# Split fp32r scores in the attention of a one-core transformer layer: query norms moved into the exponential, two scalings per head

## The chip, the cores and the metric

The kernel runs on one core of a Trainium2 chip. The metric is the device time of one launch in microseconds (us); the kernel before has a median of 1211.46 us over three runs (1211.04 to 1212.08).

## The reference, cut to what matters

One layer of width 2048 over 256 tokens, in float32: a norm, a sparse attention with 16 query heads in 4 groups that share a key head, an output projection, a feed-forward of 8192 and a gated addition. What the change touches is the attention:

```python
q = rms_norm(q.reshape(bsz, seq, H, dk), q_g)            # H = 16, dk = 128
k_c = rms_norm(compress(kv(k_c), ...), k_g[0])           # 15 compressed keys
sc = einsum(qb, k_c) * scale;  pc = masked_softmax(sc)   # scale = dk ** -0.5
ss = einsum(qb, kg) * scale;   sw = einsum(qb, kwb) * scale
return gb[0] * o_cmp + gb[1] * o_slc + gb[2] * o_win
```

With 256 tokens both the selected and the window branch see all earlier tokens, so each head has three softmaxes: one over 15 compressed keys, and two causal ones over up to 256 keys (`slc` and `win`, the "two branches").

## The kernel before, in words

Every large product is computed in fp32r, a one-pass float32 format, with both operands split into a high and a low part: three products (hi by hi, hi by lo, lo by hi) stand for one exact one. The weights come in **units** of 128 x 1024 numbers, by SyncE's queue into 8 raw buffers. For each unit ScalarE makes the high part (`split_hi`, L585) and VectorE the low part (`split_lo`, L899) in one of 4 split buffers, and TensorE uses it in two **half-units** (`half_unit`) of six products of 512 columns (`tile_product`, L1373). ScalarE may write unit u only when TensorE has used unit u-4, VectorE follows ScalarE, and TensorE waits for VectorE (`lo_done`).

All other work is written by hand between the units. `split_hi` and `split_lo` are generators: the body under `for k in split_hi(...)` runs on its engine *after* unit k is split and *before* unit k+1. Each engine works strictly in its written order, so what waits in the body holds the next split up.

The attention stands in the projections of the query groups (C_Q+1 to C_Q+3) and in the first 16 units of the output projection. `attention_step(g, s)` says what TensorE does ahead of half-unit s (0 to 15) while group g's queries are prepared and group g-1's heads run; n is 4(g-1):

- s=0, 4: `head_scores` of heads n+2, n+3; s=1, 5, 9: `head_transpose` of n+1 to n+3; s=3, 7, 11: `head_output` of n+1 to n+3
- s=6: the eight transposes of group g's queries, after `normed` (VectorE's scaling by the query norm, `staged_scale`); s=7: `cmp_scores(g)`; s=8, 12: `head_scores` of n+4, n+5; s=13: `head_transpose(n+4)`; s=15: `head_output(n+4)`

Queries `q_t` and keys `k_t` are plain float32. A head's scores are one product of 256 and one of 512 columns (L1512, L1513), each recorded as two MATMULs. Then VectorE masks and takes the maxima (`head_max`, L1058, L1062), ScalarE takes four exponentials (`head_exp`, L662), VectorE scales them by gate over sum (`head_scale`, L1075), TensorE transposes them, ScalarE and VectorE copy them out (`head_pt`: L670, L672 on ScalarE, L1108, L1109 on VectorE), TensorE multiplies with the values (`head_output`, L1560 to L1564), and ScalarE and VectorE split the result (`head_o`: L677, L1114). `cmp_scores` gives the compressed scores of a group, and VectorE's `cmp_max` (L1081, L1084, L1085) masks them, takes maxima and subtracts; the counter `cmp_read` at its end releases ScalarE's `cmp_softmax` and TensorE's `head_scores`. `head_transpose(hh)` waits for `s_scaled` (the end of `head_scale(hh)`) and for `o_done` (the end of `head_o(hh-1)` on VectorE). POOL raises mean squares to the power -1/2 (`power`).

The order on the two engines in the second half of a group's eight units:

```python
# ScalarE, L782-L794                 # VectorE, L1240-L1262
k == 4: head_pt(n+2); head_exp(n+3)  k == 4: head_max(n+3); head_pt(n+2); queries_out(g)
k == 5: head_o(n+2); cmp_softmax(g)  k == 5: head_scale(n+3); head_o(n+2); cmp_max(g)
k == 6: head_pt(n+3); head_exp(n+4)  k == 6: head_max(n+4); head_pt(n+3); cmp_scale(g)
k == 7: head_o(n+3)                  k == 7: head_scale(n+4); head_o(n+3)
```

Later, results are turned by a round trip through DRAM into four buffers (`turned`: the memory of q_t, v_slc, v_win and p_t).

## Time and profile before

| | |
|---|---|
| median of three runs | 1211.46 us (1211.04 to 1212.08) |
| profiled execution, its own time | 1213.45 us |
| its span, first to last instruction | 1211.7 us |
| TensorE (PE) busy | 1203.0 us, 99% |
| VectorE (DVE) busy | 736.6 us, 61% |
| ScalarE (ACT) busy | 573.5 us, 47% |
| granted TensorE clock over the span | 1.00 of full speed |

The attention spans about 184 to 364 us. Times in the trace count from the first instruction. A MATMUL's own duration is longer than what it adds to a row of them, because they are pipelined; what one costs is read from the starts of the instructions around it.

### The profile page before, as it was taken

What the parts mean: (1) busy time and instruction counts of PE and PEld (TensorE: products, weight loads), DVE (VectorE), ACT (ScalarE), POOL (GpSimd) and SP (SyncE); (2) the same over time, 40 slices, a digit from 0 to 9 for tenths busy, and PEclk for the clock granted to TensorE, in tenths of its full rate; (3) what the DMA queues carried; (4) which work ended last, traced back from release to release, by engine and by line L of the source; (5) the groups of instructions that cost most, each with busy time, mean ns of one, the idle gap of its engine ahead of it and who ended that gap; (6) DMA issues with size and microseconds to landing.
All of it is one profiled execution on the core that took longest, in us unless ns stands there. A gap on an engine that the chain in (4) does not pass through costs nothing.

```text
span 1211.7 us, 15271 instructions
## 1 busy us (share of the span) xinstructions
PE 1203.0 (99%) x5499; PEld 992.8 (82%) x5499; DVE 736.6 (61%) x1002; ACT 573.5 (47%) x785; POOL 75.0 (6%) x62
## 2 busy tenths in 40 slices
PE   8999999999999999999999999999999999999998
PEld 7888888888888888888888888888888888888886
DVE  5677646887767646654456564555655457576554
ACT  6554443555455545443344443444433445455442
POOL 1000000000000002100011100011100012000000
PEclk9999999999999999999999999999999999999999
DMA  9677665333338776776667766677666776786661
GB/s 328 199 217 220 179 192 152 112 114 104 105 122 273 216 231 200 242 244 192 192 207 241 247 218 194 179 245 246 222 205 195 206 244 210 250 264 204 210 203 57
DMA packets 159645, 244.85 MB, mean 202 GB/s; under 512 B 11124, under 2 KB 54504, under 8 KB 159592
## 3 DMA queue, kind: packets, MB, share of 16 engines
q1 hardware_dynamic: 159048, 243.63, 64.2%
q8 instruction: 32, 0.52, 0.2%
q10 hardware_dynamic: 544, 0.52, 0.2%
q14 instruction: 21, 0.17, 0.0%
HBM read 230.48 MB, written 13.63 MB: 201 GB/s over the span
## 4 chain that ended last, share of the span: by engine, by line
PE 92%; DVE 4%; DMA 2%; issue 1%; ACT 1%; SPq 0%; ACTq 0%; DVEq 0%
PE acc L1373 84%; DVE w_split L899 1%; PE tr L1429 1%; PE sc L1513 1%; PE sc L1477 1%; PE sc L1526 1%; PE sc L1512 0%; PE sc L1418 0%; PE tr L1418 0%; DMA v_slc<-turn_dram 0%; DMA h<-in_x_dram 0%; DMA q_t<-turn_dram 0%; DMA turn_dram<-junk 0%; DMA turn_dram<-s 0%; PE tr L1561 0%
## 5 line engine op out<-in xcount | busy, mean ns | idle before, releaser
L899 DVE TENSOR_TENSOR w_split<-w_raw,w_split 128x1024 fp32r<-128x1024 f32 x411 | 510.1, 1250 | 396.7 <-ACT w_split L585 396.1
L585 ACT ACTIVATE w_split<-w_raw 128x1024 fp32r<-128x1024 f32 x411 | 431.5, 1058 | 417.8 <-PE acc L1373 413.5
L1373 PE MATMUL acc<-w_split,a_hi 128*128 128x512 f32 x1916 | 598.8, 394 | 0.0
L1373 PE MATMUL acc<-w_split,b_split 128*128 128x512 f32 x1920 | 443.3, 391 | 0.2 <-DVE w_split L899 0.2
L1373 PEld LDWEIGHTS acc<-w_split,b_split 128*128 128x128 f32 x1920 | 359.3, 188 | 77.2 <-issue 2.9
L1373 PEld LDWEIGHTS acc<-w_split,a_hi 128*128 128x128 f32 x1916 | 357.0, 188 | 77.7 <-issue 4.9
L1373 PE MATMUL acc<-w_split,a_lo 128*128 128x512 f32 x958 | 373.5, 390 | 0.0
L1373 PEld LDWEIGHTS acc<-w_split,a_lo 128*128 128x128 f32 x958 | 180.1, 188 | 38.0
L547 POOL TENSOR_TENSOR stage<-stage 128x512 f32<-128x512 f32 x32 | 50.4, 1595 | 559.2 <-ACT stage L593 559.2
L593 ACT ACTIVATE stage<-acc,rstd 128x512 f32<-128x512 f32 x48 | 30.2, 680 | 11.9 <-PE acc L1373 10.2
L533 POOL TENSOR_TENSOR rs<-ms,minus_half 128x8 f32<-128x8 f32 (+1 forms) x7 | 17.4, 2493 | 252.6 <-DVE ms L962 252.6
L662 ACT ACTIVATE s<-s,nmx 128x128 f32<-128x128 f32 (+1 forms) x64 | 28.3, 445 | 5.9 <-DVE nmx L1062 5.9
L1121 DVE TENSOR_TENSOR h<-acc,h 128x512 f32<-128x512 f32 x40 | 25.8, 686 | 7.1 <-PE acc L1373 7.1
L670 ACT ACTIVATE p_t<-tr 128x512 f32<-128x512 f32 x16 | 9.6, 599 | 42.6 <-PE tr L1541 42.6
L1058 DVE CUSTOM_DVE_ANT_0 s<-sc,causal 128x128 f32<-128x128 f32 (+1 forms) x64 | 19.0, 353 | 0.0
L533 POOL TENSOR_TENSOR rstd<-ms,minus_half 128x2 f32<-128x2 f32 x3 | 3.0, 997 | 226.6 <-DVE ms L954 226.6
L1075 DVE TENSOR_SCALAR s<-s,cf 128x128 f32<-128x128 f32 (+1 forms) x64 | 16.1, 317 | 0.6
L1513 PE MATMUL sc<-k_t,q_t 128*128 128x512 f32 x32 | 16.3, 592 | 0.0
L628 ACT ACTIVATE junk_act<-h 128x512 f32<-128x512 f32 x24 | 15.1, 629 | 1.4 <-DVE h L1121 1.0
L913 DVE SCALAR_TENSOR_TENSOR a_lo<-tr,const_t,a_hi 128x256 fp32r<-128x256 f32 x24 | 10.1, 478 | 8.5 <-ACT a_hi L606 8.5
L606 ACT ACTIVATE a_hi<-tr,const_t 128x256 fp32r<-128x256 f32 x24 | 9.5, 474 | 11.1 <-PE tr L1429 11.1
L622 ACT ACTIVATE b_split<-v_win 128x1024 fp32r<-128x1024 f32 x4 | 4.2, 1060 | 18.9 <-DMA v_win<-turn_dram 18.9
(189 smaller groups left out, 504.8 us busy)
## 6 DMA issues: line engine op xcount, KB each, us to landing
w_raw<-in_mlp_w_dram SPq DMA_DIRECT2D x256, 512.0 KB, 4.4
w_raw<-in_nsa_w_in_dram SPq DMA_DIRECT2D x79, 512.0 KB, 4.4
w_raw<-in_nsa_w_out_dram SPq DMA_DIRECT2D x32, 512.0 KB, 3.8
w_raw<-in_ple_w_gate_dram SPq DMA_DIRECT2D x32, 512.0 KB, 4.3
turn_dram<-junk SPq DMA_DIRECT2D x44, 128.0 KB, 3.8
turn_dram<-s SPq DMA_DIRECT2D x44, 128.0 KB, 3.9
w_raw<-in_nsa_cmp_w_dram SPq DMA_DIRECT2D x8, 512.0 KB, 5.1
q_t<-turn_dram SPq DMA_DIRECT2D x12, 256.0 KB, 4.5
```

What stands on the lines that cost most here:

```text
L533: nc.gpsimd.tensor_tensor(o, ms[0:rows, 0:cols], minus_half[0:rows, 0:cols], ALU.pow).then_inc(rs_ready, 1)
L547: nc.gpsimd.tensor_tensor(stage[:, t], stage[:, t], stage[:, t], ALU.mult)\
L585: nc.scalar.activation(w_hi[:, u % SPLIT], w_raw[:, u % RAW], ACT.Copy).then_inc(hi_done, 1)
L593: nc.scalar.activation(dst(t), acc[c % 2][t][:], func, scale=scale[:, t:t + 1])\
L628: ins = nc.scalar.activation(junk_act[:], h[:, t, n * NW:(n + 1) * NW], ACT.Square, accum_out=ss[:, norm, t, n:n + 1])
L662: last = nc.scalar.activation(s, s, ACT.Exp, bias=nmx[:, par, 2 * t + br:2 * t + br + 1], scale=SCALE, accum_out=sm[:, par, 2 * t + br:2 * ...
L899: nc.vector.tensor_tensor(w_lo[:, u % SPLIT], w_raw[:, u % RAW], f32(w_hi[:, u % SPLIT]), ALU.subtract).then_inc(lo_done, 1)
L1058: ins = nc.vector.tensor_tensor_reduce(out=masked, in0=scores, in1=mask, scale=1.0, scalar=-3e38, op0=ALU.add, op1=ALU.max, accum_out=mx[: ...
L1075: ins = nc.vector.tensor_scalar(s, s, cf[:, par, 2 * t + br:2 * t + br + 1], None, ALU.mult)
L1121: nc.vector.tensor_tensor(cols, acc[c % 2][t][:], cols, ALU.add).then_inc(acc_read[c % 2][t], 1)
L1373: last = nc.tensor.matmul(acc[c % 2][t][:], xs[:, kt, toks], ws[:, u % SPLIT, m * NW:(m + 1) * NW], start=(kt == 0 and n == 0), stop=(kt = ...
L1513: nc.tensor.matmul(sc[1][:], q_t[:, j, P:SEQ], keys, start=True, stop=True).then_inc(s_full, 1)
```

## The change

- **Split scores.** Keys become `k_hi` (ScalarE, `keys_hi`) and `k_low` (VectorE); queries become `q_hi` (ScalarE, `queries_hi`, on ScalarE at k == 4 between `head_pt(n+2)` and `head_exp(n+3)`) and `q_lo` (VectorE, `queries_out`, now after ScalarE). A head's scores are three fp32r products of 256 and three of 512 columns. Compressed keys are split side by side (`kc_split`, 16 columns each part): per token half and head one product of 32 columns and one of 16.
- **Queries unscaled.** `staged_scale` of the queries goes. POOL's `power` writes `q_scale` (the norm and the factor in one), which is the scale operand of the exponentials, a pointer to one number a partition in place of a constant. `cmp_max` has five operations in place of three: one adds the second part of the scores, one multiplies by `q_scale`.
- **Order.** `cmp_scores` moves from s=7 to s=8, `head_scores(n+4)` from s=8 to s=9 (behind `head_transpose(n+3)`).
- **Two scalings.** `head_scale` has one multiplication per token half, with the factors broadcast, in place of one per half and branch.
- **Copies.** The 128x256 copy of `head_pt` moves from VectorE to ScalarE.
- **Output product.** The compressed product (fp32r) comes first in its sum, the float32 ones after it.
- **Memory.** Columns 1024 on of x go to `x_late`, whose place `k_low` and then `h_late` take; they are loaded again (1 MB) for `h_late` in the output projection, after all scores. The turns use two buffers in place of four. Small tiles share memory with others.

```diff
@@ keys and queries, ScalarE @@
+            def keys_hi(r, br):
+                for b in range(2):
+                    act.wait_ge(tr_full[b], r + 1)
+                    nc.scalar.activation(k_hi[:, 2 * b:2 * b + 2, :, br],
+                                         tr[b][:].rearrange("p (g t s) -> p g t s", g=2, t=TT), ACT.Copy,
+                                         scale=const_t[:, GAIN_K + 1 + br:GAIN_K + 2 + br]).then_inc(tr_hi[b], 1)
+            def queries_hi(g):
+                for b in range(2):
+                    act.wait_ge(tr_full[b], q_set(g) + 1)
+                    nc.scalar.activation(q_hi[:, 2 * b:2 * b + 2], tr[b][:].rearrange("p (m s) -> p m s", m=2), ACT.Copy,
+                                         scale=const_t[:, GAIN_Q:GAIN_Q + 1]).then_inc(tr_hi[b], 1)
@@ head_exp @@
-                                                    scale=SCALE, accum_out=sm[:, par, 2 * t + br:2 * t + br + 1])
+                                                    scale=q_scale[:, hh // HPG % 2, t, hh % HPG:hh % HPG + 1],
+                                                    accum_out=sm[:, par, 2 * t + br:2 * t + br + 1])
@@ head_pt, ScalarE @@
+                nc.scalar.activation(p_t[:, hh % 2, NW:NW + SEQ], tr[1][:, 0:SEQ], ACT.Copy)
@@ ScalarE, body of unit k @@
-                    if k == 4 and g:
-                        head_pt(n + 2)
-                        head_exp(n + 3)
+                    if k == 4:
+                        if g:
+                            head_pt(n + 2)
+                        if g < G:
+                            queries_hi(g)
+                        if g:
+                            head_exp(n + 3)
@@ queries_out, VectorE @@
-                    dve.wait_ge(tr_full[b], q_set(g) + 1)
-                    nc.vector.tensor_scalar(q_t[:, 2 * b:2 * b + 2], tr[b][:].rearrange("p (m s) -> p m s", m=2),
-                                            const_t[:, GAIN_Q:GAIN_Q + 1], None, ALU.mult).then_inc(tr_done[b], 1)
+                    dve.wait_ge(tr_hi[b], hi_sets(q_set(g)))
+                    nc.vector.scalar_tensor_tensor(
+                        out=q_lo[:, 2 * b:2 * b + 2], in0=tr[b][:].rearrange("p (m s) -> p m s", m=2),
+                        scalar=const_t[:, GAIN_Q:GAIN_Q + 1], in1=f32(q_hi[:, 2 * b:2 * b + 2]),
+                        op0=ALU.mult, op1=ALU.subtract).then_inc(tr_done[b], 1)
@@ head_scale @@
-                    for br in range(2):
-                        s = (s1 if t else s0)[:, par, br]
-                        ins = nc.vector.tensor_scalar(s, s, cf[:, par, 2 * t + br:2 * t + br + 1], None, ALU.mult)
+                    s = (s1 if t else s0)[:, par]
+                    ins = nc.vector.tensor_tensor(s, s, c4[:, t, :, None].to_broadcast([P, 2, (t + 1) * P]), ALU.mult)
@@ cmp_max @@
+                link(nc.vector.tensor_tensor(cmp_s[:], scores[:, :, :, 1, 0:N_CMP], cmp_s[:], ALU.add))
                 rows = cmp_s[:].rearrange("p t j n -> p (t j) n")
                 link(nc.vector.reduce_max(cmp_m[:], rows, axis=AXX))
-                nc.vector.tensor_tensor(rows, rows, cmp_m[:, :, None].to_broadcast([P, TT * HPG, N_CMP]),
-                                        ALU.subtract).then_inc(cmp_read, 1)
+                link(nc.vector.tensor_tensor(rows, rows, cmp_m[:, :, None].to_broadcast([P, TT * HPG, N_CMP]),
+                                             ALU.subtract))
+                dve.wait_ge(rs_ready, 5 + g)
+                own = q_scale[:, g % 2].rearrange("p t j -> p (t j)")[:, :, None]
+                nc.vector.tensor_tensor(rows, rows, own.to_broadcast([P, TT * HPG, N_CMP]), ALU.mult)\
+                  .then_inc(cmp_read, 1)
@@ head_pt, VectorE @@
-                nc.vector.tensor_copy(p_t[:, hh % 2, NW:NW + SEQ], tr[1][:, 0:SEQ])
@@ VectorE, body of unit k @@
-                        if g < G:
-                            staged_scale(4 + g)
@@ head_scores @@
-                keys = k_t[:, g].rearrange("p t b s -> p (t b s)")
-                nc.tensor.matmul(sc[0][:, 0:SEQ], q_t[:, j, 0:P], keys[:, 0:SEQ], start=True, stop=True)
-                nc.tensor.matmul(sc[1][:], q_t[:, j, P:SEQ], keys, start=True, stop=True).then_inc(s_full, 1)
+                for t, cols in ((0, SEQ), (1, NW)):
+                    for n, (qs, ks) in enumerate(three_terms(q_hi, q_lo, *keys(g))):
+                        last = nc.tensor.matmul(sc[t][:, 0:cols], qs[:, j, t * P:(t + 1) * P], ks[:, 0:cols],
+                                                start=(n == 0), stop=(n == 2))
+                last.then_inc(s_full, 1)
@@ cmp_scores @@
-                        nc.tensor.matmul(sc[1][:, at:at + N_CMP], q_t[:, j, t * P:(t + 1) * P], kc_t[:, g],
+                        nc.tensor.matmul(sc[1][:, at:at + 2 * CSTEP], q_hi[:, j, toks],
+                                         kc_split[:, g].rearrange("p b n -> p (b n)"), start=True, stop=False)
+                        last = nc.tensor.matmul(sc[1][:, at:at + CSTEP], q_lo[:, j, toks], kc_split[:, g, 0],
+                                                start=False, stop=True)
@@ attention_step @@
-                        pe.wait_ge(normed, 3 + g)
+                        staged(C_Q + g)
                         transpose_set(q_set(g), from_stage)
-                    if s == 7:
+                    if s == 8:
                         cmp_scores(g)
-                    if s in (8, 12):
+                    if s in (9, 12):
                         head_scores(n + 4 + (s - 8) // 4)
@@ SyncE, output projection @@
+                    if n == 2 and k == 3:
+                        sp.wait_ge(s_full, H)
+                        sp.dma_start(h_late[:], x_v[:, :, 2 * NW:]).then_inc(x_again, 16)
```

## Rows read from the trace of the kernel before

**Rows 1.** First part of the page: busy us (share) by engine.
```profile
PE 1203.0 (99%) x5499; PEld 992.8 (82%) x5499; DVE 736.6 (61%) x1002; ACT 573.5 (47%) x785; POOL 75.0 (6%) x62
```
**Rows 2.** Waits: who waited for whom, total us, times, longest.
```profile
PEld tr L1429 <- DVE p_cmp L1109: 1.2, 3, 0.4
```
**Rows 3.** Chain in order of time: start, us, what; fp32r products without other work.
```profile
80.43 3.83 PE sc L1477 x32
...
241.57 2.75 PE acc L1373 x12
```
**Rows 4.** Timeline (start, us, engine, what): TensorE around the scores of head 2.
```profile
216.32 0.39 PE L1373 MATMUL acc<-w_split,a_lo 128*128 128x512 f32 x1
...
218.31 0.40 PE L1373 MATMUL acc<-w_split,a_lo 128*128 128x512 f32 x1
```
**Rows 5.** Timeline of group 0, queries to the transposes of head 0.
```profile
195.91 1.40 DVE L995 TENSOR_SCALAR q_t<-tr,const_t 128x512 f32<-128x512 f32 x2
...
197.00 0.40 PE L1373 MATMUL acc<-w_split,a_lo 128*128 128x512 f32 x1
...
199.37 0.28 DVE L1081 TENSOR_TENSOR cmp_s<-sc,cmp_neg 128x120 f32<-128x120 f32 x1 [0.94 <-PE sc L1526]
199.69 0.28 DVE L1084 TENSOR_REDUCE cmp_m<-cmp_s 128x8 f32<-128x120 f32 x1
...
208.78 1.01 DVE L1075 TENSOR_SCALAR s<-s,cf 128x128 f32<-128x128 f32 x4
...
210.11 0.27 PE L1540 MATMUL tr<-ident,s 128*128 128x128 f32 x1
```
**Rows 6.** Timeline of group 1, query transposes to the transposes of head 4.
```profile
230.72 0.40 ACT L662 ACTIVATE s<-s,nmx 128x128 f32<-128x128 f32 x1 [0.86 <-DVE nmx L1062]
...
231.39 0.66 PE L1429 MATMUL tr<-ident,stage 128*128 128x128 f32 x4 [0.16 <-DVE p_cmp L1109]
...
231.81 0.70 PE L1373 MATMUL acc<-w_split,a_hi 128*128 128x512 f32 x2
...
232.49 1.05 ACT L585 ACTIVATE w_split<-w_raw 128x1024 fp32r<-128x1024 f32 x1
...
233.57 1.23 DVE L899 TENSOR_TENSOR w_split<-w_raw,w_split 128x1024 fp32r<-128x1024 f32 x1 [0.73 <-ACT w_split L585]
...
234.70 1.85 PE L1526 MATMUL sc<-kc_t,q_t 128*128 128x15 f32 x16
...
236.59 0.28 DVE L1081 TENSOR_TENSOR cmp_s<-sc,cmp_neg 128x120 f32<-128x120 f32 x1
...
241.19 0.17 DVE L1062 TENSOR_SCALAR nmx<-mx 128x4 f32<-128x4 f32 x1
...
244.77 1.23 DVE L899 TENSOR_TENSOR w_split<-w_raw,w_split 128x1024 fp32r<-128x1024 f32 x1 [0.24 <-ACT w_split L585]
...
247.44 0.42 DVE L1114 TENSOR_TENSOR b_split<-tr,b_split 128x256 fp32r<-128x256 f32 x1
...
249.65 0.27 PE L1540 MATMUL tr<-ident,s 128*128 128x128 f32 x1
```
**Rows 7.** Groups of ScalarE by line and shape: busy us, mean ns | idle before.
```profile
L593 ACT ACTIVATE stage<-acc,rstd 128x512 f32<-128x512 f32 x48 | 30.2, 680 | 11.9 <-PE acc L1373 10.2 <-POOL rstd L533 1.4
...
L606 ACT ACTIVATE a_hi<-tr,const_t 128x256 fp32r<-128x256 f32 x24 | 9.5, 474 | 11.1 <-PE tr L1429 11.1
...
L677 ACT ACTIVATE b_split<-tr 128x256 fp32r<-128x256 f32 x12 | 4.6, 386 | 13.5 <-PE tr L1564 13.5
```
**Rows 8.** Groups of VectorE by line and shape.
```profile
L1351 DVE TENSOR_TENSOR h<-stage,h 128x512 f32<-128x512 f32 x7 | 4.8, 692 | 0.2
...
L1351 DVE TENSOR_TENSOR h<-stage,h 128x256 f32<-128x256 f32 x2 | 0.8, 425 | 0.1
```
**Rows 9.** Timeline at the last head (15).
```profile
353.88 0.42 DVE L1114 TENSOR_TENSOR b_split<-sc,b_split 128x256 fp32r<-128x256 f32 x1
...
354.79 0.27 PE L1540 MATMUL tr<-ident,s 128*128 128x128 f32 x1
```

More of the change, by code:

```diff
@@ L153, in sem @@
             return ctx.enter_context(nc.semaphore(name))
-        h = sb("h", [P, TT, D])
+        h_early = sb("h_early", [P, TT, 2 * NW])
+        with nc.sbuf_tensor("x_late", [P, TT, 2 * NW], F32) as x_late:
+            pass
+        with nc.sbuf_tensor("k_low", [P, G // 2, 2 * NW], F32R) as k_low:
+            pass
+        h_late = sb("h_late", [P, TT, 2 * NW])
         a_hi = sb("a_hi", [P, KT, SEQ], F32R)
@@ L178, in trunk_layer @@
         p_cmp = sb("p_cmp", [P, 2, SEQ], F32R)
+        kc_rows, kc_sq = (p_t[0:N_CMP, b, 0:NW] for b in range(2))
         mx = sb("mx", [P, 2, 4])
@@ L279, in trunk_layer @@
         turn_out = [sem(f"turn_out{b}") for b in range(2)]
-        turn_in = [sem(f"turn_in{b}") for b in range(4)]
+        turn_in = [sem(f"turn_in{b}") for b in range(2)]
         turned_hi = sem("turned_hi")
@@ L284, in trunk_layer @@
         blocks = (junk[:], s1[:].rearrange("p a b s -> p (a b s)"))
-        turned = (q_t[:].rearrange("p j s -> p (j s)"), v_slc[:].rearrange("p t n -> p (t n)"),
-                  v_win[:].rearrange("p t n -> p (t n)"), p_t[:].rearrange("p a n -> p (a n)")[:, 0:2 * NW])
+        turned = [v[:].rearrange("p t n -> p (t n)") for v in (v_slc, v_win)]
         block = ctx.enter_context(nc.Block())
@@ L291, in f32, with columns, keys, three_terms @@
             return ap.bitcast(F32)
+        def columns(late, n, t, at=0, cols=NW):
+            at += n % 2 * NW
+            return (late if n >= 2 else h_early)[:, t, at:at + cols]
+        def keys(g):
+            return (k_hi[:, g].rearrange("p t b s -> p (t b s)"), k_low[:, g // 2, g % 2 * NW:(g % 2 + 1) * NW])
+        def three_terms(x_hi, x_lo, y_hi, y_lo):
+            return (x_hi, y_hi), (x_hi, y_lo), (x_lo, y_hi)
         def out_bank(hh):
@@ L504, in _ @@
             nc.gpsimd.memset(fold[:], 0.0)
+            nc.gpsimd.memset(f32(kc_split[:]), 0.0)
             nc.gpsimd.memset(causal[:], 0.0)
@@ L721, in _ @@
                     hidden(0)
+                if k == 7:
+                    keys_hi(R_KS, 0)
             for k in split_hi(CMP_FIRST[1], CMP_UNITS):
@@ L944, in h_rows @@
             def h_rows(n):
-                return lambda t: h[:, t, n * NW:(n + 1) * NW]
+                return lambda t: columns(h_late, n, t)
             def mean_square(n, norm):
@@ L1194, in _ @@
                     dve.wait_ge(kct_full, 1)
-                    nc.vector.tensor_scalar(kc_t[:].rearrange("p g n -> p (g n)"), sc[1][:, 0:G * N_CMP],
-                                            const_t[:, GAIN_K:GAIN_K + 1], None, ALU.mult).then_inc(kct_ready, 1)
+                    own = sc[1][:, 0:G * N_CMP].rearrange("p (g n) -> p g n", n=N_CMP)
+                    kc_hi, kc_lo = (kc_split[:, :, part, 0:N_CMP] for part in range(2))
+                    link(nc.vector.tensor_scalar(kc_hi, own, const_t[:, GAIN_K:GAIN_K + 1], None, ALU.mult))
+                    nc.vector.scalar_tensor_tensor(out=kc_lo, in0=own, scalar=const_t[:, GAIN_K:GAIN_K + 1],
+                                                   in1=f32(kc_hi), op0=ALU.mult, op1=ALU.subtract)\
+                      .then_inc(kct_ready, 1)
                 if k == 6:
@@ L1449, in h_split_by, with from_h @@
                     split_by(r, k % 2)
-            def from_h(n):
-                return lambda t, b: h[:, t, n * NW + b * P:n * NW + (b + 1) * P]
+            def from_h(n, late=h_late):
+                return lambda t, b: columns(late, n, t, b * P, P)
             def staged(c):
@@ L1524, in cmp_scores @@
                     for j in range(HPG):
-                        at = (t * HPG + j) * N_CMP
-                        last = nc.tensor.matmul(sc[1][:, at:at + N_CMP], q_t[:, j, t * P:(t + 1) * P], kc_t[:, g],
-                                                start=True, stop=True)
+                        at, toks = (t * HPG + j) * 2 * CSTEP, slice(t * P, (t + 1) * P)
+                        nc.tensor.matmul(sc[1][:, at:at + 2 * CSTEP], q_hi[:, j, toks],
+                                         kc_split[:, g].rearrange("p b n -> p (b n)"), start=True, stop=False)
+                        last = nc.tensor.matmul(sc[1][:, at:at + CSTEP], q_lo[:, j, toks], kc_split[:, g, 0],
+                                                start=False, stop=True)
                 last.then_inc(cmp_full, 1)
```

106 lines of the change are left out of this document (58 added, 48 removed).

## The prediction

> **What bounds the kernel now.** First the page: TensorE is busy 99% of the span, VectorE 61%, ScalarE 47% [rows 1], so a microsecond less of products is a microsecond less of time, unless TensorE then waits. Second the waits: in the attention the only wait of TensorE that the list charges to another engine more than once is for VectorE's `p_cmp`, 1.2 us in three places [rows 2]. Third the timelines of one group [rows 5, 6], because a busy share says nothing of order. They show how late VectorE's signals come: head 0's scalings end at 208.78 + 1.01 = 209.79 and TensorE takes them at 210.11, 0.32 us later [rows 5]; head 4's transposes start at 249.65, 1.8 us after what they wait for (247.44 + 0.42) [rows 6]; at the last head 0.49 us are left (354.30 to 354.79) [rows 9]. So TensorE is the bound, but a second bound, the ring ScalarE, VectorE, ScalarE, runs 0.3 to 1.8 us behind it. The change takes work off TensorE and puts work on that ring.
>
> **Prices on TensorE.** Fp32r products of 512 columns follow at 2.75/12 = 0.229 us, those of 256 at 3.83/32 = 0.120 [rows 3]; a half-unit is 6 x 0.229 = 1.375. A head's float32 scores stand between two starts that would be three products apart: 218.31 - 216.32 - 3 x 0.229 = 1.30 us [rows 4]. After: 3 x (0.120 + 0.229) = 1.05. That saves 0.25 a head, 16 x 0.25 = 4.0 us. The compressed scores are 16 records of 15 columns in 1.85 us, 0.11 each [rows 6]; after, they are 16 products of 32 or 16 columns, each again with its own 128 weight columns. I take no change (as nearest row; 0.120 each would add 0.13 us a group). The order of the output product and the head's fp32r part cost the same in either place: 0.
>
> Two small waits shrink. In group 0 TensorE's compressed scores come at 199.37 less 16 records, about 0.2 us later than the product at 197.00 would let them, because VectorE's q_t ends at 197.31 [rows 5]; one half-unit more lies between now, so 0.2 goes. The three waits for `p_cmp` (0.4 each) [rows 2]: the copy ahead of `p_cmp` on VectorE goes, which is some 0.34 earlier (425 ns for such a size [rows 8], less the overlap), while TensorE comes 0.25 earlier. 0.4 - 0.34 + 0.25 leaves 0.3; the `staged_scale` ahead of them goes too, so I take 0.15 left and 0.7 us gained of 1.2. TensorE's gains: 4.0 + 0.7 + 0.2 = 4.9 us.
>
> **Prices on the ring.** `cmp_max` gets two operations; such linked ones start 0.32 us apart [rows 5], so +0.63. The exponentials get a pointer for their scale beside the pointer for their bias. No row has two pointers. A copy of 256 columns takes 474 ns with a pointer and 386 without [rows 7], so one pointer costs 0.088; the second costs 0 (both read at once) to 0.088. I take 0.088, as the first did: 4 x 0.088 = +0.35 a head. The Trainium skill, "ScalarE: Activation LUTs", section "What ACT_TABLE_LOAD costs", says that each pointer operand adds about 93 ns; by it alone the term would be 0.37, and no run so far shows a second pointer. `head_scale`: four multiplications take 1.01 us [rows 5]; two tensor-by-tensor ones of 256 and 512 columns take 0.425 + 0.692 less some 0.09 of overlap [rows 8], 1.03: no gain. The 128x256 copy costs ScalarE 0.386 less the overlap, 0.30. `queries_hi` is two passes of 512 columns at 0.68 [rows 7], ahead of `head_exp(n+3)`. `queries_out` keeps its length.
>
> **Group 0, after.** From the start of `cmp_max` to TensorE's transposes of head 0 TensorE needed 210.11 - 199.37 = 10.74 us [rows 5]. One half-unit (1.38) now lies ahead of `cmp_max`, and two heads' scores are 0.25 shorter: 8.86. The ring needed 209.79 - 199.37 = 10.42: `cmp_max`, compressed exponential, ScalarE's split of unit 6, VectorE's, `head_max`, `head_exp`, both splits of unit 7, `head_scale`. Unit 7 stands in it because each engine splits it after the body of unit 6. After: 10.42 + 0.63 + 0.35 = 11.40, and 0.06 to TensorE. TensorE waits 11.46 - 8.86 = 2.6 us (part of it at head 0's scores, for `cmp_read`, the rest at the transposes).
>
> **Groups 1 to 3, after.** From the end of the query transposes to those of head 4 TensorE takes 249.65 - 231.81 = 17.84; the same steps in another order, less two times 0.25, make 17.34. The ring from the landing of the transposes (231.39 + 0.66 = 232.05) [rows 6]:
> - `queries_hi`, second bank, 0.04 + 0.68 - 0.09 (overlap) = 0.63. Before, `head_exp` ran at 230.72 and waited for no queries.
> - `head_exp`, 232.49 - 230.72 = 1.77, + 0.35 = 2.12; ScalarE's split to VectorE's split, 233.57 - 232.49 = 1.08
> - VectorE's split, `head_scale`, `head_o` to `cmp_max`: 236.59 - 233.57 = 3.02
> - `cmp_max` to the end of the next head's `nmx`, 241.36 - 236.59 = 4.77, + 0.63 = 5.40
> - 0.04 + `head_exp` 2.12 + ScalarE's split 1.08; VectorE's split to the end of `head_o`, 247.86 - 244.77 = 3.09; 0.06 to TensorE
>
> The sum: 0.63 + 2.12 + 1.08 + 3.02 + 5.40 + 2.16 + 1.08 + 3.09 + 0.06 = 18.64. TensorE's clock starts at 231.81, 0.24 before the ring's at 232.05, so it arrives at 17.34 - 0.24 = 17.10. It waits 18.64 - 17.10 = 1.54 us a group, 4.6 us for three. Behind the waiting transposes stand all later products, so the wait is lost time.
>
> **The last head.** 0.49 us were left [rows 9]. The copy (0.30) and the pointer (0.35) make the ring 0.65 longer, which is 0.2 of wait at least. The ring's round for one head also becomes about as long as TensorE's (some 8.85 us each), so lateness carried in from earlier is not made up; I take 0.9, with 0.2 to 1.1 as bounds.
>
> **The sum.** Gains 4.9; waits 2.6 + 4.6 + 0.9 = 8.1; net +3.2 us. Against the profiled execution's own 1213.45 (1.75 beyond its span of 1211.7) this is 1216.6; the median of the runs is 1.99 below that execution, so the forecast is 1211.46 + 3.2 = 1214.7.
>
> **What is costed at nothing, and its cover.** ScalarE's `keys_hi` (two times 1.3 us) runs at k = 7 while TensorE is over two half-units from the next unit; without that cover it would cost up to 1.3 each. The second load of x is twice a unit's load, issued when all scores are made, and VectorE needs it only when the third output chunk ends, some 14 units (38 us) later; SyncE's queue waits for the last scores at the time at which it would wait for a split buffer anyway, and eight raw buffers cover it. Two turn buffers in place of four: VectorE writes the blocks of turn n after it has read turn n-1, so the new owner is never early. The extra clearing of `kc_split` on POOL delays only TensorE's first filler products, which end before the loads of x.
>
> **Rivals.**
> - *The second pointer is free.* Every ring passes one `head_exp` (group 0) or two (groups 1 to 3). Waits: 2.6 - 0.35, 3 x (1.5 - 0.7), 0.5: 5.2. Net +0.3, 1211.8, no difference. For it: no row shows two; against it: the 88 ns of one.
> - *TensorE's saving comes through (the other side).* The ring has cover that my sums do not see: VectorE or ScalarE pick up their splits earlier, and the waits total under 2.5 us, from where on it is faster by over 0.2%. With none, -4.9, 1206.6. For it: TensorE is the bound today with 0.3 to 1.8 us to spare. Against it: group 0's wait alone is 2.6, built of measured stretches.
> - *A transfer or a turn gets in the way.* The reload or the halved turns make one wait of about 3 us more: 1217.7. For it: SyncE's queue is one and in order; against it, the covers above.
>
> **Chances.** My forecast 0.60, the free pointer 0.25, the saving 0.12, the transfer 0.03. About 0.2%, 2.4 us, is what a measurement tells from no change. The forecast's own range is 1213.2 to 1217.2 (last head 0.2 to 1.1, up to 0.3 us a ring for hops that I read 0.1 off); nearly all of it is slower, the free pointer is no difference. So slower 0.60, same 0.28, faster 0.12. The range reaches down past the free pointer: 1210.5 to 1217.5.
>
> **What would show it.** Right: in the list of waits TensorE's transposes of heads 0, 4, 8, 12 wait for VectorE's scaling or `b_split`, head 0's over 1.5 us; the first piece of `head_exp`, 0.40 us now [rows 6], takes 0.49; scores cost 1.05 us between starts; `head_scale` stays at 1.0 us. Wrong if that piece still takes 0.40, or if TensorE's waits in the attention total under 5 us.

## Result, and the profile after

Five runs of the changed kernel have a median of 1216.89 us (1215.83 to 1218.31); the kernel before, over five runs as well, 1212.01 (1211.04 to 1213.16). The ratio is 1.0039, with a 95% interval of 1.0028 to 1.0051: slower by 4.9 us by the medians, 3.4 to 6.2 by the interval. Forecast were 1214.7 us, which is 3.2 more than the 1211.46 of the first three runs of the kernel before, and a range of 1210.5 to 1217.5.

The profiled execution took 1215.83 us, with a span of 1213.7. The busy times of the page answer [rows 1]:

```profile
PE 1199.8 (99%) x5531; PEld 994.5 (82%) x5531; DVE 729.2 (60%) x959; ACT 589.7 (49%) x813; POOL 71.5 (6%) x63
```

TensorE is busy 3.2 us less than before, ScalarE 16 us more, and yet the time grew. The list of waits, TensorE's own lines (who waited for whom, total us, times, longest), answers [rows 2]:

```profile
PE tr L1605 <- DVE b_split L1172: 2.3, 4, 0.6
PE sc L1659 <- POOL ident L537: 2.2, 1, 2.2
PE tr L1605 <- DVE s L1131: 2.0, 1, 2.0
PE sc L1574 <- DVE cmp_s L1146: 1.2, 3, 0.4
PE tr L1490 <- DMA h_early<-in_x_dram: 1.0, 1, 1.0
PE tr L1625 <- DVE p_cmp L1167: 0.3, 2, 0.2
```

Before, one wait of the attention was listed, 1.2 us for `p_cmp` ahead of the query transposes. It is gone. In its place stand four groups: the transposes of heads 0, 4, 8, 12 and 15 wait for the scaling (L1131) or for the low part of the output (L1172, `o_done`), the scores of heads 4, 8 and 12 for the compressed maximum (L1146), and the outputs of heads 3, 7 and 11 for `p_cmp` (L1167; the list has two of these three, the starts show all). These figures are idle time only. A MATMUL's record is longer than the time it adds to a row of them, so what a wait costs is read from the starts, as the timeline of group 1 shows (start, us, engine, line, what, idle before); it answers the second half of [rows 6]:

```profile
240.16 0.28 DVE L1146 TENSOR_TENSOR cmp_s<-cmp_s,q_scale 128x120 f32<-128x120 f32 x1
240.47 0.30 ACT L724 ACTIVATE cmp_s<-cmp_s 128x120 f32<-128x120 f32 x1 [4.36 <-DVE cmp_s L1146]
...
240.59 0.36 PE L1574 MATMUL sc<-k_hi,q_split 128*128 128x256 f32 x1 [0.39 <-DVE cmp_s L1146]
...
240.68 1.04 ACT L612 ACTIVATE w_split<-w_raw 128x1024 fp32r<-128x1024 f32 x1
...
241.76 1.23 DVE L950 TENSOR_TENSOR w_split<-w_raw,w_split 128x1024 fp32r<-128x1024 f32 x1 [1.32 <-ACT w_split L612]
...
242.90 0.28 DVE L1112 CUSTOM_DVE_ANT_0 s<-sc,causal 128x128 f32<-128x128 f32 x1
...
244.13 0.16 DVE L1117 SCALAR_TENSOR_TENSOR nmx<-mx,q_scale 128x4 f32<-128x4 f32 x1
...
244.33 0.49 ACT L703 ACTIVATE s<-s,nmx,q_scale 128x128 f32<-128x128 f32 x1 [1.59 <-DVE nmx L1117]
...
245.88 0.59 ACT L703 ACTIVATE s<-s,nmx,q_scale 128x256 f32<-128x256 f32 x1
...
246.46 1.04 ACT L612 ACTIVATE w_split<-w_raw 128x1024 fp32r<-128x1024 f32 x1
...
247.54 1.23 DVE L950 TENSOR_TENSOR w_split<-w_raw,w_split 128x1024 fp32r<-128x1024 f32 x1 [1.21 <-ACT w_split L612]
...
249.29 1.02 DVE L1131 TENSOR_TENSOR s<-s,cf 128x256 f32<-128x256 f32 x2
...
249.85 0.39 PE L1434 MATMUL acc<-w_split,a_lo 128*128 128x512 f32 x1
250.23 0.42 DVE L1172 TENSOR_TENSOR b_split<-tr,b_split 128x256 fp32r<-128x256 f32 x1
...
250.79 0.30 PE L1605 MATMUL tr<-ident,s 128*128 128x128 f32 x1 [0.56 <-DVE b_split L1172]
```

The last product before head 4's transposes starts at 249.85, so they could start at 250.08; they start at 250.79, 0.71 later, and read against the same transposes without a wait, which add 0.88 us to the row of products, the place costs 0.75. Read so, each of the three full groups loses 0.65 (scores), 0.40 (output) and 0.75 (transposes), 1.8 us; group 0 loses 0.42 at head 0's scores and 2.26 at its transposes (from 208.38, the start of the last product, to 210.81, theirs); the last head 0.83: 8.9 us in all. Read the same way, the kernel before loses 1.6 us: 1.17 in the three waits for `p_cmp` and 0.4 in group 0.

The rows also show how the ring is built. ScalarE stands 4.36 us at the compressed exponential (L724), with the split of unit 6 behind it. VectorE stands 1.32 us for that split, with the maximum of head 4 (L1112) behind it. Then ScalarE takes the exponential and only after it splits unit 7 (246.46), VectorE waits 1.21 us for that, with the scaling (L1131) behind it, and TensorE waits for the scaling.

### The profile page after: what moved, and what is told of

Its sections match the earlier page's. It is cut to its first block, busy times and chain, and to the rows that moved or that the text cites. A ratio compares the mean times of both kernels' runs of the same rounds, so it can differ in the third digit from the quotient of the medians.

```text
span 1213.7 us, 15318 instructions
## 1 busy us (share of the span) xinstructions
PE 1199.8 (99%) x5531; PEld 994.5 (82%) x5531; DVE 729.2 (60%) x959; ACT 589.7 (49%) x813; POOL 71.5 (6%) x63
## 4 chain that ended last, share of the span: by engine, by line
PE 91%; DVE 5%; ACT 3%; issue 1%; DMA 0%; ACTq 0%
PE acc L1434 86%; DVE w_split L950 2%; ACT s L703 2%; ACT w_split L612 1%; PE tr L1490 1%; DVE s L1131 1%; PE sc L1538 1%; DVE s L1112 1%; PE sc L1574 1%; PE sc L1479 0%; PE tr L1479 0%; DMA h_early<-in_x_dram 0%; PE acc L1464 0%; ACT q_split L688 0%; DVE b_split L1172 0%
## 5 line engine op out<-in xcount | busy, mean ns | idle before, releaser
L703 ACT ACTIVATE s<-s,nmx,q_scale 128x128 f32<-128x128 f32 (+1 forms) x64 | 34.2, 537 | 11.9 <-DVE nmx L1117 11.9
L649 ACT ACTIVATE b_split<-v_slc 128x1024 fp32r<-128x1024 f32 x8 | 8.5, 1061 | 31.0 <-DMA v_slc<-turn_dram 31.0
L649 ACT ACTIVATE b_split<-v_win 128x1024 fp32r<-128x1024 f32 x8 | 8.5, 1060 | 26.9 <-DMA v_win<-turn_dram 26.9
L1574 PE MATMUL sc<-k_hi,q_split 128*128 128x256 f32 (+1 forms) x64 | 18.6, 343 | 1.3 <-DVE cmp_s L1146 1.2
L1112 DVE CUSTOM_DVE_ANT_0 s<-sc,causal 128x128 f32<-128x128 f32 (+1 forms) x64 | 18.9, 350 | 0.0
L560 POOL TENSOR_TENSOR q_scale<-ms,minus_half 128x8 f32<-128x8 f32 x4 | 7.5, 1862 | 175.1 <-DVE ms L1013 175.1
L1131 DVE TENSOR_TENSOR s<-s,cf 128x256 f32<-128x256 f32 (+1 forms) x32 | 16.4, 554 | 0.6
L993 DVE TENSOR_TENSOR b_split<-v_win,b_split 128x1024 fp32r<-128x1024 f32 x8 | 16.5, 2063 | 0.0
L1179 DVE TENSOR_TENSOR h_late<-acc,h_late 128x512 f32<-128x512 f32 x20 | 12.9, 686 | 3.9 <-PE acc L1434 3.9
L1179 DVE TENSOR_TENSOR h_early<-acc,h_early 128x512 f32<-128x512 f32 x20 | 12.9, 686 | 3.3 <-PE acc L1434 3.3
```

The costliest lines, as they stand in the source:

```text
L649: nc.scalar.activation(b_hi[:, 4 * j:4 * j + 4].rearrange("p m (g j) -> p m g j", j=QUAD), turned_tiles(n), ACT.Copy).then_inc(turned_hi, 1)
L703: last = nc.scalar.activation(s, s, ACT.Exp, bias=nmx[:, par, 2 * t + br:2 * t + br + 1], scale=q_scale[:, hh // HPG % 2, t, hh % HPG:hh % ...
L993: nc.vector.tensor_tensor(lo, turned_tiles(T_HID + j), f32(hi), ALU.subtract).then_inc(turned_split, 1)
L1112: ins = nc.vector.tensor_tensor_reduce(out=masked, in0=scores, in1=mask, scale=1.0, scalar=-3e38, op0=ALU.add, op1=ALU.max, accum_out=mx[: ...
L1131: ins = nc.vector.tensor_tensor(s, s, c4[:, t, :, None].to_broadcast([P, 2, (t + 1) * P]), ALU.mult)
L1179: nc.vector.tensor_tensor(cols, acc[c % 2][t][:], cols, ALU.add).then_inc(acc_read[c % 2][t], 1)
```

## Experiments

All but two start from the changed kernel; `x_before_ring` and `b_pointer` start from the kernel before. A result is given as the ratio to the kernel before in the same session, with its 95% interval, and as the difference of the two medians, which is +4.9 us for the changed kernel. **Length of the attention** is the time in the profile from the first of group 0's query transposes to the first of head 15's output products: 163.50 us before, 166.90 after. A **loss** is what a wait of TensorE adds, read from the starts as above.

| kernel | median us | ratio to before | minus before, us | attention, us |
|---|---|---|---|---|
| changed kernel | 1216.89 | 1.0039 (1.0028 to 1.0051) | +4.9 | 166.90 |
| after_again (the same) | 1217.40 | 1.0040 (1.0027 to 1.0054) | +4.8 | 168.53 |
| x_pointer | 1213.07 | 1.0004 (0.9995 to 1.0013) | +0.7 | 163.41 |
| x_order | 1220.47 | 1.0071 (1.0057 to 1.0084) | +8.1 | 169.00 |
| x_copy | 1217.54 | 1.0040 (1.0027 to 1.0054) | +5.1 | 167.21 |
| x_exp_late | 1211.56 | 0.9994 (0.9985 to 1.0003) | -0.6 | 162.54 |
| x_cmp_late | 1212.31 | 1.0002 (0.9994 to 1.0011) | +0.1 | 162.92 |
| x_queries_late | 1214.87 | 1.0019 (1.0010 to 1.0028) | +2.7 | 164.77 |
| x_ring (all three) | 1208.12 | 0.9963 (0.9950 to 0.9977) | -4.3 | 158.76 |
| x_ring_pointer | 1207.73 | 0.9965 (0.9951 to 0.9978) | -4.6 | 158.38 |
| x_before_ring | 1212.58 | 1.0002 (0.9993 to 1.0011) | +0.4 | 163.48 |
| b_pointer | 1213.82 | 1.0012 (1.0003 to 1.0021) | +1.5 | 164.87 |

### The second pointer: x_pointer

```diff
@@ head_max, VectorE: nmx @@
-                nc.vector.scalar_tensor_tensor(out=nmx[...], in0=mx[...], scalar=-1.0, in1=own, op0=ALU.mult, op1=ALU.mult)
+                nc.vector.tensor_scalar(nmx[:, par], mx[:, par], -SCALE, None, ALU.mult)
@@ head_exp, ScalarE @@
-                                                    scale=q_scale[:, hh // HPG % 2, t, hh % HPG:hh % HPG + 1],
+                                                    scale=SCALE,
```

> Leaves out the queries' norm of the two scored branches: the factor of the exponential is the constant again, and its bias the maximum times that constant. Theory (the loop of scores, maximum, exponential, scaling and transposes sets the pace of the attention): each of the four exponentials of a head falls back by the 0.09 us that it gained, 0.36 us a head; the 2.68 us of waits of the first group falls by 0.36, those of the last head by 0.36, and in each of the three full groups, where four heads follow one another, by between 0.75 (the wait before the transposes of the group's last head alone) and 1.4 (four heads): 3.0 to 4.9 us in all, so 0.9960 to 0.9975 of the changed kernel's time. Rival (the second factor is hidden behind other work of ScalarE, and the waits come from the later place of the compressed scores): no more than 0.4 us in all.

Against before it went from +4.9 to +0.7 us, 4.2 less; the attention is 3.5 us shorter. The rival that the pointer is hidden falls. The groups of the exponential by shape, first of the changed kernel and then of x_pointer (busy us, mean ns, idle before):

```profile
L703 ACT ACTIVATE s<-s,nmx,q_scale 128x256 f32<-128x256 f32 x32 | 18.7, 587 | 0.0
L703 ACT ACTIVATE s<-s,nmx,q_scale 128x128 f32<-128x128 f32 x32 | 15.5, 487 | 11.9 <-DVE nmx L1117 11.9
```

```profile
L703 ACT ACTIVATE s<-s,nmx 128x256 f32<-128x256 f32 x32 | 15.8, 495 | 0.0
L703 ACT ACTIVATE s<-s,nmx 128x128 f32<-128x128 f32 x32 | 12.6, 395 | 10.1 <-DVE nmx L1116 9.8
```

A second pointer costs 92 ns at both sizes (587 - 495, 487 - 395). The Trainium skill ("ScalarE: Activation LUTs", section "What ACT_TABLE_LOAD costs") gives about 93 ns for each pointer operand; the trace agrees, for the second one too.

### The later place of the compressed scores: x_order

```diff
@@ attention_step, TensorE @@
-                    if s == 8:
+                    if s == 7:
                         cmp_scores(g)
-                    if s in (9, 12):
+                    if s in (8, 12):
```

> Compressed scores back before half unit 7 and the first head's scores back before half unit 8, one half unit (1.37 us) earlier each; all else as in the changed kernel. Theory (ring): the low parts of the queries and the five steps of the compressed maximum are then not done in time, and TensorE waits for them directly: about 0.5 us more before the compressed scores of the first group, and 0.7 to 1.4 us more before the scores of the first head of each group, less what the transposes then wait less: 1 to 3.5 us slower. Rival (the later place of the scores is itself what made the transposes of head 0, 4, 8 and 12 late): those waits shrink by up to 1.37 us each, at most 3 to 5 us faster.

It is 3.2 us slower than the changed kernel; in the profiled execution, at full clock, the attention is 2.1 us longer, and the other four have mean clocks of 0.996 and 0.997, so part of the 3.2 may be the clock (below). The later place did not make the transposes late, it gave VectorE time. TensorE's largest wait is now ahead of the scores, up to 2.7 us at once, in place of 0.4:

```profile
PE sc L1574 <- DVE cmp_s L1146: 8.0, 3, 2.7
```

### The copy: x_copy

```diff
@@ head_pt, ScalarE @@
-                nc.scalar.activation(p_t[:, hh % 2, NW:NW + SEQ], tr[1][:, 0:SEQ], ACT.Copy)
@@ head_pt, VectorE @@
+                if hh >= 2:
+                    dve.wait_ge(o_full, hh - 1)
+                nc.vector.tensor_copy(p_t[:, hh % 2, NW:NW + SEQ], tr[1][:, 0:SEQ])
```

> The 128 x 256 copy of the turned probabilities goes back to VectorE, with its wait for the output bank. Theory: ScalarE gets 0.38 us a head back and VectorE's work grows by 0.42 us in front of the low part that frees the transpose bank; both engines lie in the loop, so the sum is within 1 us of the changed kernel, and the wait of the query transposes for that bank (0.4 us a group before, gone now) comes back: 0 to 1.2 us slower. Rival (ScalarE alone sets the loop): 0.38 us a head comes off the waits, 3 us faster in all.

No difference that can be measured (+5.1 against +4.9 us). The wait of the query transposes comes back, as expected, with a loss of 0.2 to 0.3 us in each full group, and the losses total 9.2 us in place of 8.9. In this ring through both engines it does not matter which of them does a piece of similar length.

### ScalarE's order alone: x_ring

```diff
@@ ScalarE, body of unit k @@
                         if g:
                             head_pt(n + 2)
+                            head_exp(n + 3)
                         if g < G:
                             queries_hi(g)
-                        if g:
-                            head_exp(n + 3)
-                    if k == 5:
-                        if g:
-                            head_o(n + 2)
-                        if g < G:
-                            cmp_softmax(g)
+                    if k == 5 and g:
+                        head_o(n + 2)
                     if k == 6:
+                        if g < G:
+                            cmp_softmax(g)
                         if g:
                             head_pt(n + 3)
-                        if g < G:
-                            head_exp(n + 4)
-                    if k == 7 and g:
-                        head_o(n + 3)
+                    if k == 7:
+                        if g < G:
+                            head_exp(n + 4)
+                        if g:
+                            head_o(n + 3)
```

> Only ScalarE's order is changed, no instruction added or left out: the exponential of a group's first head goes behind the split of unit 7, the compressed exponential behind the split of unit 6, and the high part of the queries behind the exponential of the fourth head. Theory (in the loop ScalarE stands at a split that waits for TensorE to use an older unit, while TensorE waits for the work behind it): the waits of 5.4 us in the three full groups go nearly all, and 1 to 2 us of the first group's 2.7, so 5 to 8 us off: 0.9934 to 0.9959 of the changed kernel, below the kernel before. Rival (the loop is one of the work itself, exponentials and products in series): a split moved in front of the exponential makes it later by as much as it waited, and the time stays within 1 us or grows by up to 2 us.

It is 9.2 us faster than the changed kernel (4.9 + 4.3), 1.2 more than the most expected, and 4.3 us faster than the kernel before, though not one instruction is left out. The attention is 8.1 us shorter. The whole list of TensorE's waits in x_ring:

```profile
PE sc L1659 <- POOL ident L537: 2.2, 1, 2.2
PE tr L1490 <- DMA h_early<-in_x_dram: 1.8, 1, 1.8
PE acc L1434 <- DVE w_split L950: 0.3, 1, 0.3
PE tr L1605 <- DVE b_split L1172: 0.2, 1, 0.2
```

The first two are in the start. Read from the starts, the attention loses 0.8 us in place of 8.9: 0.4 at head 0's scores, 0.3 at head 15's transposes. The timeline at the same place of group 1:

```profile
237.31 0.28 DVE L1146 TENSOR_TENSOR cmp_s<-cmp_s,q_scale 128x120 f32<-128x120 f32 x1
...
237.51 1.22 DVE L950 TENSOR_TENSOR w_split<-w_raw,w_split 128x1024 fp32r<-128x1024 f32 x1
...
240.91 0.49 ACT L703 ACTIVATE s<-s,nmx,q_scale 128x128 f32<-128x128 f32 x1 [0.85 <-DVE nmx L1117]
...
242.83 1.22 DVE L950 TENSOR_TENSOR w_split<-w_raw,w_split 128x1024 fp32r<-128x1024 f32 x1
...
244.57 1.03 DVE L1131 TENSOR_TENSOR s<-s,cf 128x256 f32<-128x256 f32 x2
```

VectorE's low part of unit 6 now follows the compressed maximum at once (0.20 us between starts; 1.60 in the changed kernel), and that of unit 7 starts at 242.83, while ScalarE is still at the exponentials; in the changed kernel it started 3.21 us after the first of them (247.54 - 244.33), here 1.92 after.

### The three moves one by one: x_exp_late, x_cmp_late, x_queries_late

Each has one of the three moves of the diff above: `head_exp(n + 4)` to k == 7; `cmp_softmax(g)` to k == 6; `queries_hi(g)` behind `head_exp(n + 3)`.

> The first third of x_ring alone: on ScalarE the exponential of heads 0, 4, 8 and 12 goes behind the split of unit 7. Theory (VectorE's low part of unit 7 and the scaling behind it wait for a split that stands behind the exponential): the low part is then made while the exponential runs, the scaling starts about 1.2 us earlier, the 0.75 us wait before the transposes of heads 4, 8 and 12 goes, and of the 2.3 us before those of head 0 about 1.2 to 1.5 us: 3.4 to 3.8 us off the changed kernel in all; the waits for the compressed maximum (0.65 us a group) stay. Rival (the whole of x_ring's gain is one cause, the compressed exponential that holds the split of unit 6): under 1 us. Second rival: the split makes the exponential late and the transposes wait longer: slower.

> The second third of x_ring alone: on ScalarE the compressed exponential goes behind the split of unit 6. Theory (the compressed exponential waits for the compressed maximum and holds the split of unit 6, behind which VectorE makes the low part and then the maximum of head 4, 8 or 12): that maximum starts about 1 us earlier, the waits of 0.4 us before the last output and 0.75 us before the transposes in each full group go, and about 1 us of the first group's 2.3 us: 3.5 to 4.5 us off in all. The wait of TensorE for the compressed maximum itself (0.65 us a group) stays. Rival (the exponential's place alone sets the loop): under 1 us.

> The last third of x_ring alone: on ScalarE the high part of the queries goes behind the exponential of a group's fourth head. Theory (the 1.26 us of the high part stand in front of that exponential, behind which VectorE scales and then takes the compressed maximum that TensorE waits for): the 0.65 us before the first head's scores go in the three full groups, 2.0 us in all, nothing in the first group (it has no fourth head), and of the other waits up to 0.5 us a group: 1.5 to 3.5 us off. Rival (the queries' low part then comes too late for the compressed scores): a new wait there of up to 1.2 us a group, and the gain is gone.

Against the changed kernel they are 5.5, 4.8 and 2.2 us faster, in the attention 4.4, 4.0 and 2.1. The first gave about 2 us more than was expected of it (0.6 to 1 by the attention): the loss at head 0's transposes fell by 1.6, and that at head 15's, which the expectation left out, by 0.5. The other two gave about what was expected. Neither rival of a single cause holds: each move helps alone. The three together (9.2) give less than their sum (12.5), because the first two each take away much of the same losses, those at the transposes. TensorE's waits in the attention, of x_exp_late:

```profile
...
PE sc L1575 <- DVE cmp_s L1147: 1.2, 3, 0.4
PE tr L1606 <- DVE s L1132: 0.4, 1, 0.4
PE tr L1626 <- DVE p_cmp L1168: 0.3, 2, 0.2
PE tr L1606 <- DVE b_split L1173: 0.2, 1, 0.2
```

of x_cmp_late:

```profile
...
PE sc L1573 <- DVE cmp_s L1145: 1.2, 3, 0.4
PE tr L1604 <- DVE s L1130: 1.0, 1, 1.0
PE tr L1604 <- DVE b_split L1171: 0.6, 1, 0.6
```

and of x_queries_late:

```profile
PE tr L1605 <- DVE b_split L1172: 2.4, 4, 0.7
PE tr L1605 <- DVE s L1131: 2.0, 1, 2.0
PE tr L1625 <- DVE p_cmp L1167: 0.2, 1, 0.2
```

The wait for the compressed maximum goes only with the third move; those at the transposes shrink only with the first two.

### The same order in the kernel before: x_before_ring

The first two moves in the kernel before (it has no `queries_hi`).

> The kernel before, with ScalarE's exponential of heads 0, 4, 8, 12 behind the split of unit 7 and the compressed exponential behind that of unit 6 (the queries have no high part there). Theory (before the change TensorE's own work was longer than the loop of the other engines, so nothing waits on these two): the same within 0.3 us, with the p_cmp wait of 0.4 us a group still there. Rival (the new order is simply better, whatever the scores cost, and x_ring's gain says nothing of the change): 2 to 5 us faster than before.

The interval includes no change, and the attention is as long as before (163.48). So these two moves are worth nothing where TensorE's own work is the longer, and 5.5 and 4.8 us, each alone, where the ring is. (The 9.2 us of x_ring have the third move in them, which the kernel before cannot have.)

### The pointer in the kernel before, and in x_ring: b_pointer, x_ring_pointer

```diff
@@ b_pointer: kernel before, head_exp; factor holds SCALE in every row @@
-                                                    scale=SCALE, accum_out=...
+                                                    scale=factor[:], accum_out=...
```

> The kernel before with one part of the change alone: the factor of the exponential read from a tile (the same constant for every row) and not as a constant of the instruction. Theory (before, TensorE's own work is the longer one and the loop of the other engines has some slack): each exponential 0.09 us longer, 5.8 us more of ScalarE in all, and the time the same within 0.5 us; a wait of up to 0.4 us a group if the slack is smaller than that. Rival (the loop was already the bound before): the time grows by the 3.8 us that x_pointer gave back.

The theory was half wrong. The exponentials grew as in the changed kernel, those of 128 columns from 393 to 487 ns:

```profile
L663 ACT ACTIVATE s<-s,nmx,factor 128x128 f32<-128x128 f32 x32 | 15.5, 487 | 7.1 <-DVE nmx L1063 7.1
```

The time grew by 1.5 us (0.4 to 2.6 by the interval), the attention by 1.4. So the kernel before had less slack than the 0.3 to 1.8 us of [rows 5, 6, 9] suggested and than I expected of this run, but the rival falls too: the ring was not the bound all the way, since the same edit is worth 4.2 us in the changed kernel. The starts show where the cover was thin: the losses grow by 1.3 us, of which 0.5 lie at group 1's query transposes, 0.2 at the scores of each of heads 4, 8 and 12, which follow the compressed maximum, and 0.15 at head 0's transposes. At the first place the kernel before had no cover, since it already waits there for `p_cmp`; the second is a path that the prediction's readings of cover left out.

> x_ring with the constant factor of x_pointer (leaves out the queries' norm of the two scored branches). Theory (in x_ring the loop no longer sets the pace, so that shorter exponentials are hidden): of the 3.8 us that the same edit gave in the changed kernel, only what is left of waits can come, about 0.3 us before the transposes of the last head: 0 to 0.5 us below x_ring. Rival (the exponentials are on the path in any order): 3 to 4 us below x_ring.

It is 0.3 us below x_ring by the differences to before and 0.4 by the medians, with overlapping intervals, as the theory said: the instruction that is worth 4.2 us in one order is worth at most some tenths in another.

### The rest of the difference: x_order_again, after_again

The attention is 3.4 us longer after the change, the medians stand 4.9 apart.

> x_order once more, for a second profile of the same kernel. Its five executions had mean granted clocks of 0.996 to 1.000 and spans of 1215.6 (at 1.000) to 1219.6 us (at 0.996); the attention of the profiled one holds only 2.1 us more than that of the changed kernel, where the medians stand 3.6 us apart. Theory (a TensorE that waits several times within one group is granted a lower clock in some executions): an execution at 0.996 to 0.998 shows a stretch with a granted clock below 1 inside or just behind the attention, 2 to 4 us longer than the same stretch at full clock. Rival (the difference is in the transfers of the start or of the turned tiles): the clock is 1.00 in every stretch of the attention and the time is lost elsewhere.

One execution, 1224.25 us, mean clock 0.994, attention 173.61 (x_order's: 169.00, at 1.000). Of the 6.5 us between the two spans (1222.1 and 1215.6) 4.6 lie in the attention and 1.7 behind it. Two windows of x_order_again (us, busy by engine, granted clock, DMA share, GB/s):

```profile
198.00:202.00 4.00, 4.00 (x17) 3.43 (x17) 1.83 (x6) 1.25 (x2) 0.00 (x0) 0.58 0.45 131
...
240.00:244.00 4.00, 3.82 (x13) 3.18 (x14) 2.53 (x11) 1.25 (x2) 0.00 (x0) 0.63 0.09 11
```

The clock is 0.58 and 0.63 there. The first stretch comes behind a loss of 0.7 us ahead of the compressed scores and the row of their 16 short products, the second begins within the wait of 2.7 us ahead of head 4's scores; two more falls stand at 284 and 325 us, beside the same waits of groups 2 and 3, and none outside the attention. That fits the theory; the rival holds at most for the 1.7 us behind the attention, where the clock is 1.00.

> The changed kernel unaltered, for a second profile of it and a closer time. Its attention holds 3.2 us more than that of the kernel before in the one profile, the medians stand 4.7 us apart, and its five executions had mean granted clocks of 0.998 to 1.000. Theory (as in the second profile of x_order, where the granted clock fell to 0.83 to 0.93 over the ten microseconds around the waits at a group's start): the clock falls for a short while after the waits in some executions, and an execution at 0.998 has a stretch of the attention below 1.00 and about 1 to 2 us more there; the median stays at 4 to 5 us above before. Rival (the rest is the start, where the first loads differ by 1 us from run to run): the clock is 1.00 in all stretches of the attention, and further executions bring the medians to 3.5 us apart or less.

The median stays (1217.40, +4.8 us), and this profile, with a mean clock of 0.998, shows one such place. Its windows around head 0's transposes, and the middle one of them in the first profile of the changed kernel:

```profile
205.00:210.00 5.00, 3.50 (x17) 2.61 (x15) 3.26 (x10) 3.63 (x9) 0.00 (x0) 1.00 0.25 87
210.00:215.00 5.00, 4.46 (x17) 3.69 (x18) 3.22 (x12) 3.27 (x10) 0.00 (x0) 0.66 0.69 209
215.00:220.00 5.00, 5.00 (x28) 4.29 (x27) 3.71 (x8) 3.57 (x7) 0.00 (x0) 1.00 0.26 79
```

```profile
210.00:215.00 5.00, 4.19 (x23) 3.64 (x24) 3.49 (x13) 2.89 (x10) 0.00 (x0) 1.00 0.71 210
```

One microsecond of it, and the timeline of after_again:

```profile
212.00:213.00 1.00, 1.00 (x3) 0.76 (x3) 0.97 (x8) 0.68 (x3) 0.00 (x0) 0.50 0.42 55
```

```profile
208.11 0.39 PE L1434 MATMUL acc<-w_split,a_lo 128*128 128x512 f32 x1
210.54 0.33 PE L1605 MATMUL tr<-ident,s 128*128 128x128 f32 x1 [2.04 <-DVE s L1131]
...
212.62 0.63 PE L1434 MATMUL acc<-w_split,a_lo 128*128 128x512 f32 x1
213.05 1.05 PE L1434 MATMUL acc<-w_split,a_hi 128*128 128x512 f32 x2
213.91 0.63 PE L1434 MATMUL acc<-w_split,a_lo 128*128 128x512 f32 x1
```

In that execution TensorE waits until 210.54, and the clock falls 0.6 us later. At a granted clock of 0.50 three products take 213.91 - 212.62 = 1.29 us, 0.43 each, where they take 0.229 [rows 3]. The attention is 1.6 us longer than in the first profile (168.53 against 166.90).

## Why the forecast was right, point by point

**The direction and its cause** were right: TensorE's saving is real and the waits of a ring through ScalarE and VectorE take more than it gives. Both sides of that are shown, the waits in the profile, the saving by x_ring, which has nearly all of it. Neither sign of being wrong is there: the first piece of `head_exp` takes 0.49 us, and the waits of the attention cost 8.9.

| term | forecast | measured |
|---|---|---|
| scores of a head | 1.30 to 1.05 us, 4.0 in all | 1.30 to 1.06, 3.9 in all |
| `p_cmp` waits, query wait of group 0 | 0.7 + 0.2 gained | 1.17 + 0.4 |
| compressed products | 0.11 each, as before | 0.11 between starts, before and after |
| second pointer | +0.088 an exponential | +0.092 |
| two more operations of `cmp_max` | +0.63 | 0.31 to 0.32 between starts, +0.63 |
| `head_scale` | 1.01 to 1.03 | 1.02 |
| copy on ScalarE | +0.30 | 0.26 between starts |
| `queries_hi` | 0.68 a pass | 0.68 |
| waits of group 0 | 2.6 | 2.7 |
| waits of a full group | 1.54, three times | 1.8, three times |
| wait of the last head | 0.9 | 0.8 |
| sum | 8.1 - 4.9 = +3.2 | 8.9 - 5.5 = +3.4 |

**Too small** were the waits of the full groups: I summed one round of the ring against one round of TensorE, and put all the loss at the transposes. The compressed maximum, however, releases the first head's scores as well, and `p_cmp` the outputs. The loss falls at three places (scores 0.65, output 0.40, transposes 0.75), and b_pointer shows that the cover of the kernel before was thinner than my readings of 0.3 to 1.8 us. **Too large** were the `p_cmp` waits ahead of the query transposes that I thought would stay: none did. The two errors, 0.8 us of waits and 0.6 of gains, nearly cancel; that the sum comes out within 0.2 us of the attention's +3.4 is in part luck.

**Not foreseen** was about 1.5 us between the attention's +3.4 and the medians' +4.9. Two parts are seen. One is the lowered clock after group 0's wait, which added 1.6 us in the one of two profiles of the changed kernel that has it. The other is 0.35 us outside the span (1215.83 - 1213.7 = 2.1, against 1.75 before; also 2.1 in x_ring). The mean clock is 0.998, as in that profile, in five of the changed kernel's ten executions, and never below 0.999 in the 73 of the kernel before whose clock is on record. But the median of these five is 1217.42 us and that of the other five 1217.01, so the clock is not shown to make up the rest. The profiles cannot settle it either: their spans stand only 2.0 us apart (1213.7 and 1211.7), because in the changed kernel's the attention starts 1.1 us earlier (193.81 against 194.91) and what lies behind it is 0.4 shorter. The cause of the second part and of the rest was not tested.

**The range.** The measured 1216.89 us lies within it by 0.6. Its upper part is not worked out: with the terms named (0.2 more at the last head, up to 0.3 in each of five rings: group 0, three full groups, the last head) the forecast reaches 1214.7 + 0.2 + 1.5 = 1216.4, not 1217.2. The median of the kernel before had also moved up by 0.55 us, from 1211.46 to 1212.01. Taken as differences, +4.9 us were measured where +3.2 were forecast.

**The rivals.** The free pointer fell by x_pointer and by the durations. The saving that comes through was wrong for this order of ScalarE, and is what x_ring then shows: -4.3 against the -4.9 named as its limit. The transfers did not show: in the changed kernel's list no wait of TensorE outside the start is for a DMA.

**Costed at nothing.** `keys_hi`, the reload of x, the two turn buffers and the clearing on POOL left no new wait in the list of TensorE (its wait for POOL in the start is 2.2 us; 2.1 before). They were not tested by themselves.

## What to carry to other kernels

A busy share of 99% says which engine is the bound, not by how much: here the second bound was under 2 us behind, and work taken off the first and put on the second cost 4.9 us. When an engine waits in its written order, look at what stands behind the waiting instruction: a split of the next weights behind an exponential cost 5.5 us, and moving it ahead cost nothing in the kernel before, where it was not needed. Price an added operand or operation only together with the order that it stands in: the same pointer was worth 4.2, 1.5 and 0.4 us in the changed kernel, in the one before and in x_ring.

## What the runs showed of the hardware

- A short wait can cost time beyond itself. After TensorE had waited some 2.2 us (208.34 to 210.54) the granted clock fell in one execution to 0.66 over the stretch from 210 to 215 us and the products came 0.43 us apart, the 1.2 GHz level, against 0.229 at full clock, 2.4 GHz; after the same wait in another execution it stayed at 1.00. The Trainium skill ("TensorE: Matmul & The Clock Gate", section "Wait — 56ns, not 53.3ns?") gives 426.7 and 215.7 ns between starts of 512 columns at the two levels; the trace agrees with the first (0.43 us), and shows 0.229 for the second, which holds here.
- A second pointer operand of an ACTIVATE costs about as much as the first did (88 ns [rows 7]): 92 ns at 128 and at 256 columns.
- Fp32r products get cheaper with fewer columns only down to a floor: 512 columns 0.229 us, 256 columns 0.120 [rows 3], but 32 and 16 columns 0.111 each, as much as 15 columns in float32 did. What bounds them was not tested.
